# Softmax attentions by head pairs, and a regrouped tail of the recurrence, in an eight-layer transformer kernel

## The chip, the cores and the metric

The program runs on one NeuronCore of one Trainium2 chip. The metric is device microseconds of the whole kernel, one launch. Before the change the median of three timed runs is 3063.12 us (3058.28 to 3063.68).

## The reference

Two stacks of layers act on x of 256 tokens by 1024 features, in float32. The four layers of the first stack are `x += ffn/2; x += mixer; x += ffn/2`, each with an RMS norm; the mixers are, in this order, a gated recurrence (HGRN2), a neighbourhood attention (NA), a latent attention (MLA) and the recurrence again. The second stack has a linear recurrence, a gated convolution ffn, a stick-breaking attention and another ffn. The change touches the first stack's mixers:

```python
# NA, 16 heads of 64; a row is 64 tokens, T = 4 rows, so every query sees all 256 keys
s = einsum(q_r, k_blk) * scale
s = where(col_mask, s + bias, NEG_INF)      # bias = rpb by row and column offset
p = softmax(s);  o = einsum(p, v)
# MLA, 16 heads, 96 query/key features, 64 value features, q and k RMS-normed and rotated
s = einsum(q_b, k) * scale;  p = softmax(s);  o = einsum(p, v)
# HGRN2, 8 heads of 128: a decayed causal attention, forward and backward
o = rms_norm(o, g_norm) * silu(g);  y = o @ w_out
```

## The kernel before

Matmuls by weights are split in three (`three`, L621 to L623): weights and activations are each cut into a high part in fp32r and a low remainder. Weights stream by units of 128x1024 through six raw buffers (SP queue); ScalarE makes the high part of a unit (L1246) and VectorE the low part (L1747), into seven split buffers. Both engines follow a hand-written order: `splits(tile)` and `ahead(n)` say up to which unit they go before the next piece of their other work, and each engine runs strictly in the order of its program. All dependences are semaphores. PSUM has eight banks; 0 to 3 are called Wk and 4 to 7 Y, and Y also collects the output of a sublayer.

`hgrn` works on four pairs of heads. In a pair, nine scores (`score`, L874) run along a ladder of decay levels: TensorE makes the score of level i, VectorE doubles the decayed keys and queries (`double`, L1986) and keeps part of the score (`keep`, L1997), ScalarE copies the keys (`facing_keys`, L1419), then the score of the next level can run. Beside the first three pairs TensorE has the input products of the next pair (`half_product`), one half after each score. The last pair has none; there the output product of the pairs 0 and 1 stands (`pair_out`, four halves after the scores 3 to 6), and behind the ladder `output`, `squares_summed`, pair 2, and after the norm (`normed`, L2004 and L2007) and its split (L1767, L1769) pair 3 in `last_tile`.

`na` makes eight units of q and k (`f_product`), each followed by `mean_squares` (L938) and by `flip` (L981), a matmul that reverses the order of the 64 partitions of each bias block; VectorE copies it back (L2109), GpSimd then adds the column mask per head (L573). Four products for v follow, then `attention`. `mla` is alike, without bias; its last part is eight `queries` with `query_squares`.

`attention` goes head by head on TensorE: scores of head i (L944, two matmuls), the four 128x128 transposes of head i-2 (L960), values of head i-3 (L971, two matmuls onto 64 partitions of a bank that two heads share). Fp32 matmuls show as two records each, transposes as one. VectorE, per head: in NA scale and bias (L2120), maximum (L2084), its negation (L2085), reciprocal of the sum of the head before (L2077), the multiplication of that head's 256x256 exponentials by it (L2079, twice 128x256), and every second head the split of the output (L1767, L1769). ScalarE: the copy of the transposed probabilities (L1487) and the exponentials with their sum (L1496). `w_out` waits for the last head's split.

## Time and profile before

| | |
|---|---|
| median of 3 timed runs | 3063.12 us (3058.28 to 3063.68) |
| profiled execution | 3055.57 us, span 3053.8 us |
| PE busy, share of the span | 93% |
| DVE, ACT, POOL | 66%, 47%, 3% |
| granted TensorE clock, mean | 0.969 |
| DMA | 478 MB, 157 GB/s |

PE is TensorE, DVE VectorE, ACT ScalarE, POOL GpSimd. The profile is of one execution. Its page has the busy time by engine and the chain of work that ended last; the trace behind it can be asked for the instructions of a stretch in order of time, for who waited for whom, and for busy time and granted clock by stretch. A granted clock of 1.00 is 2.4 GHz, 0.50 is 1.2 GHz. Times in the rows are microseconds from the start of the span. The recurrence runs from about 228 to 445 us and again from about 1933 to 2150, NA from 820 to 994, MLA's attention from 1472 to 1519.

### The profile page before, as it was taken

How to read it: one execution, taken by the hardware profiler on the slowest of the kernel's cores; microseconds unless marked ns; L12 is line 12 of the kernel's file. 1: busy time of each engine (PE TensorE's matmuls, PEld its weight loads, DVE VectorE, ACT ScalarE, POOL GpSimd, SP SyncE). 2: the span in 40 equal slices, each digit the busy share in tenths (PEclk: the TensorE clock that was granted, in tenths of full speed). 3: DMA queues.
4: the chain of work that ended last, by engine and by line, in shares of the span. 5: the costliest groups of instructions: out<-in, count | busy, mean ns of one | idle time of the engine just before them, and what ended most of it. 6: DMA issues, size and time to landing. Idle time of an engine off the chain costs nothing.

```text
span 3053.8 us, 46734 instructions
## 1 busy us (share of the span) xinstructions
PE 2855.1 (93%) x19701; PEld 2639.7 (86%) x19701; DVE 2002.9 (66%) x2615; ACT 1426.9 (47%) x1904; POOL 98.7 (3%) x148
## 2 busy tenths in 40 slices
PE   7999979999988999999999999997999699896998
PEld 6999869999975999998799999996999599794897
DVE  5667766565657666557665665776656677746777
ACT  4445544444444544445554444554444444453443
POOL 0000000000002000001100000000000100000000
PEclk9999999999999999999999999998999899997999
DMA  7654326675541565553256566432664456442562
GB/s 227 188 161 138 112 82 215 186 207 186 159 145 49 184 184 183 182 167 93 94 181 186 166 200 186 132 125 69 199 185 154 138 173 200 152 156 65 166 192 98
DMA packets 404726, 478.41 MB, mean 157 GB/s; under 512 B 16555, under 2 KB 331653, under 8 KB 404517
## 3 DMA queue, kind: packets, MB, share of 16 engines
q1 hardware_dynamic: 400944, 467.33, 48.8%
q0 software_dynamic: 1776, 6.77, 0.8%
q8 instruction: 155, 2.54, 0.3%
q10 hardware_dynamic: 1796, 1.33, 0.1%
q14 instruction: 55, 0.44, 0.0%
HBM read 474.32 MB, written 1.05 MB: 156 GB/s over the span
## 4 chain that ended last, share of the span: by engine, by line
PE 82%; DVE 10%; ACT 4%; issue 3%; ACTq 0%; DVEq 0%
PE Wk L621 17%; PE Wk L623 16%; PE Wk L622 16%; PE Y L621 9%; PE Y L622 9%; PE Y L623 9%; DVE w_lo L1747 2%; DVE work L1986 1%; ACT w_hi L1246 1%; PE Y L971 1%; PE Y L874 1%; PE Y L726 1%; PE Wk L944 1%; PE Wk L960 0%; PE Wk L874 0%
## 5 line engine op out<-in xcount | busy, mean ns | idle before, releaser
L1747 DVE TENSOR_TENSOR w_lo<-ring,w_hi 128x1024 fp32r<-128x1024 f32 (+2 forms) x910 | 1070.4, 1200 | 690.1 <-ACT w_hi L1246 643.7
L621 PE MATMUL Wk<-xT_hi,w_hi 128*128 128x256 f32 x4320 | 1233.3, 285 | 21.0 <-DVE xT_lo L1786 17.7
L623 PE MATMUL Wk<-xT_hi,w_lo 128*128 128x256 f32 x4320 | 1225.6, 284 | 0.0
L622 PE MATMUL Wk<-xT_lo,w_hi 128*128 128x256 f32 x4320 | 1225.6, 284 | 0.0
L1246 ACT ACTIVATE w_hi<-ring 128x1024 fp32r<-128x1024 f32 (+1 forms) x894 | 906.8, 1039 | 645.0 <-PE Wk L623 431.7
L621 PEld LDWEIGHTS Wk<-xT_hi,w_hi 128*128 128x128 f32 x4320 | 832.2, 193 | 28.2 <-issue 14.8
L622 PEld LDWEIGHTS Wk<-xT_lo,w_hi 128*128 128x128 f32 x4320 | 832.4, 193 | 4.7 <-issue 0.9
L623 PEld LDWEIGHTS Wk<-xT_hi,w_lo 128*128 128x128 f32 x4320 | 831.9, 193 | 0.0
L621 PE MATMUL Y<-w_hi,hid_hi 128*128 128x512 f32 x904 | 353.5, 391 | 4.3 <-DVE hid_lo L1840 4.3
L622 PE MATMUL Y<-w_lo,hid_hi 128*128 128x512 f32 x904 | 352.1, 389 | 0.0
L623 PE MATMUL Y<-w_hi,hid_lo 128*128 128x512 f32 x904 | 350.9, 388 | 0.0
L621 PEld LDWEIGHTS Y<-w_hi,hid_hi 128*128 128x128 f32 x904 | 170.1, 188 | 37.6 <-DVE hid_lo L1840 5.2
L623 PEld LDWEIGHTS Y<-w_hi,hid_lo 128*128 128x128 f32 x904 | 169.8, 188 | 35.8
L622 PEld LDWEIGHTS Y<-w_lo,hid_hi 128*128 128x128 f32 x904 | 170.2, 188 | 30.8
L1315 ACT ACTIVATE hid_hi<-work 128x512 fp32r<-128x512 f32 x112 | 70.8, 632 | 241.9 <-DVE work L1838 241.9
L621 PE MATMUL Y<-w_hi,xT_hi 128*128 128x512 f32 (+1 forms) x288 | 108.8, 378 | 31.9 <-DVE xT_lo L1769 15.6
L1840 DVE TENSOR_TENSOR hid_lo<-work,hid_hi 128x512 fp32r<-128x512 f32 x112 | 77.6, 693 | 78.3 <-ACT hid_hi L1315 78.3
L623 PE MATMUL Y<-w_hi,xT_lo 128*128 128x512 f32 (+1 forms) x288 | 104.9, 364 | 0.0
L622 PE MATMUL Y<-w_lo,xT_hi 128*128 128x512 f32 (+1 forms) x288 | 104.9, 364 | 0.0
L621 PEld LDWEIGHTS Y<-w_hi,xT_hi 128*128 128x128 f32 x288 | 56.9, 197 | 43.9 <-DVE xT_lo L1769 18.5
L1419 ACT ACTIVATE work<-work 128x512 f32<-128x512 f32 x56 | 38.0, 678 | 108.5 <-DVE work L1986 108.5
L1986 DVE TENSOR_TENSOR work<-work 128x512 f32<-128x512 f32 x112 | 79.2, 754 | 12.4 <-PE Wk L874 10.5
(283 smaller groups left out, 2829.1 us busy)
## 6 DMA issues: line engine op xcount, KB each, us to landing
ring<-in_ffn_w_gu SPq DMA_DIRECT2D x352, 512.0 KB, 4.4
ring<-in_ffn_w_down SPq DMA_DIRECT2D x224, 512.0 KB, 4.4
ring<-in_ffn_w_up SPq DMA_DIRECT2D x96, 512.0 KB, 5.9
ring<-in_hg_w_in SPq DMA_DIRECT2D x80, 512.0 KB, 3.6
ring<-in_na_w_in SPq DMA_DIRECT2D x24, 512.0 KB, 4.5
ring<-in_hg_w_out SPq DMA_DIRECT2D x16, 512.0 KB, 3.6
ring<-in_lru_w_in SPq DMA_DIRECT2D x16, 512.0 KB, 4.4
ring<-in_kv_w SPq DMA_DIRECT2D x16, 512.0 KB, 4.5
```

The source lines that it names most:

```text
L621: pe.matmul(o, l_hi, r_hi, start=first, stop=False)
L622: pe.matmul(o, l_hi, r_lo, start=False, stop=False)
L623: return pe.matmul(o, l_lo, r_hi, start=False, stop=last)
L726: mm = pe.transpose(part_bank(tt, n)[:, k * P:(k + 1) * P], x[:, tt, a:a + P], ident)
L874: mm = pe.matmul(o[:, (2 * hh + st) * P:(2 * hh + st + 1) * P], dk, dq, start=True, stop=True)
L944: mm = pe.matmul(o[:, tt * T:(tt + 1) * T], q_of(i)[:, tt * P:(tt + 1) * P], k_of(i), start=True, stop=True)
L1246: act.activation(*both[-1], ACT.Copy).then_inc(hi_done, 1)
L1315: act.activation(hid_hi[:, h, :], ff_hid[:, h, :], ACT.Copy).then_inc(hidden_high, 1)
L1419: act.activation(hg_dk[:, i % 2, :].rearrange("p (n h b) -> p n h b", h=2, b=P >> l), facing(Q, l, 0), ACT.Copy).then_inc(dk_ready, 1)
L1747: ins = dve.tensor_tensor(l, r, h.bitcast(F32), ALU.subtract)
L1840: dve.tensor_tensor(hid_lo[:, h, :], ff_hid[:, h, :], hid_hi[:, h, :].bitcast(F32), ALU.subtract)\
L1986: dve.tensor_tensor(a, a, other_block(l, which), ALU.mult) .then_inc((k_doubled, q_doubled)[which], 1)
```

## The change

Attention. A new `softmax_attention` takes the place of `attention` in NA and MLA. VectorE no longer multiplies the exponentials: it makes a 128x128 diagonal of the inverse sums (the identity times the reciprocal), two per head. TensorE then multiplies the exponentials, as stationary operand, by the diagonal, which turns and scales at once, four real fp32 matmuls where four transposes stood. Scores and values go by pairs of heads, alternating between the two. The order on TensorE is: scores of pair g, values of pair g-2, turning of the two heads of pair g-1. The score banks are four (0, 1, 6, 7), the exponentials and the turned copies have four buffers. The maximum is negated by the reduction itself. The first pair's scores, maxima and exponentials move ahead of the last input products (NA: behind the second v product; MLA: ahead of the last queries). `w_out` starts its first half when seven of eight splits are done.

NA's bias. The flip matmuls and the copies are gone. The queries are stored in reverse order of tokens within 128, the bias load and the column mask are adapted, and the split of the output writes in reverse again.

Recurrence. The four halves of the output product of the pairs 0 and 1 go after the scores 0, 2, 4 and 6 of the last pair, in the order (0,0), (1,0), (0,1), (1,1), and the weight units are reordered for it. The split of pair 0 moves to pair 2 (into another tile), of pair 1 to level 0 and of pair 2 to level 5. The last pair's weight splits are spread over the levels, three units of the next sublayer are split ahead of the last norm, and VectorE doesn't split any more between it and the residual. In the other pairs the weight split of a level is moved ahead of the other work of that level. Squares of pair 2 move ahead by some instructions.

```diff
-MS_BANKS = (4, 4, 4, 2)
+A_BANKS = (0, 1, 6, 7)
+MS_BANKS = (4, 4, 0, 2)
+HALVES_LAST = (0, 0, 1, 1, 2, 2, 3, 4, 5)
 LEVELS = 8
 SCORES = LEVELS + 1
 HALVES_AHEAD = 4
@@ -61,8 +63,8 @@
 
 class Const:
...
-                    t_product(*out_of(t0, j), first=j == 0)
+                    if j == 0 and subs[s][0] in ("na", "mla"):
+                        for n in range(2):
+                            pe.wait_ge(s_saved, saves_before(s) + 7 + n)
+                            y_half(out_of(t0, j), n, first=True)
+                    else:
+                        t_product(*out_of(t0, j), first=j == 0)
...
                     pe.wait_ge(o_split, Q0 + j + 1)
-                    if j == 0 and n == 0:
-                        pe.wait_ge(g_saved, Q0 + HG_PAIRS)
-                        pe.wait_ge(o_ready, Q0 + HG_PAIRS - 1)
-                    y_half(out_of(base[s] + 5 * HG_PAIRS, j), n, first=j == 0)
+                    if j == 0:
+                        pe.wait_ge(*((o_ready, Q0 + HG_PAIRS - 1) if n else (g_saved, Q0 + HG_PAIRS)))
+                    t = base[s] + 5 * HG_PAIRS
+                    a = (t + j, pair_of(hid_hi, j), pair_of(hid_lo, j)) if j < 2 else out_of(t, j)
+                    y_half(a, n, first=j == 0)
...
-                        if last and 3 <= i < 7:
-                            pair_out((i - 3) // 2, (i - 3) % 2)
+                        if last and i in (0, 2, 4, 6):
+                            pair_out(i // 2 % 2, i // 4)
...
+            def scores_of_pair(g, q_of, k_of):
+
+                for tt in range(TT):
+                    for h in (2 * g, 2 * g + 1):
+                        mm = pe.matmul(bank(A_BANKS[h % 4])[:, tt * T:(tt + 1) * T],
+                                       q_of(h)[:, tt * P:(tt + 1) * P], k_of(h), start=True, stop=True)
+                        if tt:
+                            mm.then_inc(s_psum, 1)
+
+            def softmax_attention(s, q_of, k_of, at_v, at_p, at_pT):
+
+                h0, s0, pairs = heads_before(s), saves_before(s), NA_H // 2
+
+                def turned(h):
+
+                    pe.wait_ge(s_prob, 2 * (h0 + h + 1))
+                    if h >= 2:
+                        pe.wait_ge(s_turned_sb, h0 + h - 1)
+                    for kk in range(TT):
+                        for tt in range(TT):
+                            mm = pe.matmul(bank(2 + h % 2)[:, kk * T + tt * P:kk * T + (tt + 1) * P],
+                                           at_p[:, h % 4, tt, kk * P:(kk + 1) * P], inv_diag[:, h % 2, tt, :],
+                                           start=True, stop=True)
+                    mm.then_inc(s_turned, 1)
+
+                def values(g):
+
+                    pe.wait_ge(s_turned_sb, h0 + 2 * g + 2)
+                    if g >= 2:
+                        pe.wait_ge(s_saved, s0 + g - 1)
+                    for kk in range(TT):
+                        for hh in range(2):
+                            h = 2 * g + hh
+                            mm = pe.matmul(bank(4 + g % 2)[64 * hh:64 * hh + 64, 0:T], at_v[:, kk, 64 * h:64 * h + 64],
+                                           at_pT[:, h % 4, kk, :], start=(kk == 0), stop=(kk == 1))
+                            if kk:
+                                mm.then_inc(s_out, 1)
+
+                for g in range(pairs + 2):
+                    if 1 <= g < pairs:
+                        scores_of_pair(g, q_of, k_of)
+                    if g >= 2:
+                        values(g - 2)
+                    if 1 <= g <= pairs:
+                        turned(2 * g - 2)
+                        turned(2 * g - 1)
...
-                    flip(i - 1)
-                pe.wait_ge(na_flipped, NA_H // 2)
                 for j in range(4):
                     if j >= 2:
                         pe.wait_ge(p_v, v0 + TT * (j - 1))
                     v_product(base[s] + 8 + j, bank(4 + j % 2))
-                pe.wait_ge(p_out, u0 + 8)
+                    if j == 1:
+                        pe.wait_ge(p_out, u0 + 8)
+                        scores_of_pair(0, part(na_q), part(na_k))
                 pe.wait_ge(p_v, v0 + 8)
-                attention(s, NA_H, part(na_q), part(na_k), NA_D, na_v, na_p, na_pT)
-                pe.wait_ge(s_saved, saves_before(s) + 8)
+                softmax_attention(s, part(na_q), part(na_k), na_v, na_p, na_pT)
                 w_out(s, base[s] + 12)
...
+                    if i == 7:
+                        pe.wait_ge(k_fin, 8)
+                        scores_of_pair(0, q_of, k_of)
                     queries(i)
                     if i < 2:
                         key_squares(2 + i)
                     if i:
                         query_squares(i - 1)
-                pe.wait_ge(k_fin, 8)
-                for h in range(3):
-                    scores_of(h, q_of, k_of)
                 query_squares(7)
                 pe.wait_ge(q_fin, 8)
-                attention(s, MLA_H, q_of, k_of, MLA_V, ml_v, ml_p, ml_pT, ahead=3)
-                pe.wait_ge(s_saved, saves_before(s) + 8)
+                softmax_attention(s, q_of, k_of, ml_v, ml_p, ml_pT)
                 w_out(s, t0 + 15)
...
+                        if last and i == 1:
+                            squares_of(p_ - 1)
                         if i < LEVELS - 1:
                             facing_keys(p_, i + 1)
                         if i in (0, LEVELS - 1, LEVELS):
                             keep(p_, i)
                         if i == 1:
                             g_sigmoid(Q)
-                        if p_ and i == 3 - 2 * last:
+                        if not last:
+                            ahead(HALVES_AHEAD + 10 * (p_ + 1) + i, s)
+                        if p_ and i == 3 and not last:
                             squares_of(p_ - 1)
                         if p_ and i == 5 - 3 * last:
                             roots(p_ - 1)
@@ -1463,7 +1530,9 @@
                                 one_minus(Q + 1)
                             elif i == LEVELS:
                                 save_values(p_ + 1)
-                        ahead(HALVES_AHEAD + 10 * (p_ + 1) + i, s)
+                        else:
+                            ahead(HALVES_AHEAD + 38 + HALVES_LAST[i], s)
+                ahead(10 * HG_PAIRS + 10, s, over=True)
                 squares_of(HG_PAIRS - 1)
                 roots(HG_PAIRS - 1)
...
+                for g in range(1, pairs + 1):
+                    if g < pairs:
+                        exps(2 * g)
+                    turned(2 * g - 2)
+                    turned(2 * g - 1)
+                    if g < pairs:
+                        exps(2 * g + 1)
...
                 def split_pair(pp):
                     dve.wait_ge(o_ready, Q0 + pp + 1)
-                    split_out(2 * pp, 2, hg_o[:, pp, :], (o_high, Q0 + pp + 1), o_split)
+                    if pp >= 2:
+                        split_out(2 * pp, 2, hg_o[:, pp, :], (o_high, Q0 + pp + 1), o_split)
+                        return
+                    dve.tensor_copy(hid_hi[:, pp, :], hg_o[:, pp, :]).then_inc(o_high, 1)
+                    dve.wait_ge(o_high, Q0 + pp + 1)
+                    dve.tensor_tensor(hid_lo[:, pp, :], hg_o[:, pp, :], hid_hi[:, pp, :].bitcast(F32), ALU.subtract)\
+                        .then_inc(o_split, 1)
 
                 splits(base[s] + 2)
                 dve.wait_ge(r_ready, norms_before(s) + 1)
@@ -2035,13 +2138,14 @@
                             save_g(p_)
                         elif i == 2:
                             gate_of(p_)
-                        if last and i in (1, 2):
-                            split_pair(i - 1)
+                        if p_ == HG_PAIRS - 2 and i == 5:
+                            split_pair(0)
+                        if last and i in (0, 5):
+                            split_pair(1 + i // 5)
                         if p_ and i == 6 - 3 * last:
                             normed(p_ - 1)
-                            if last:
-                                split_pair(2)
                         if not last:
+                            ahead(HALVES_AHEAD + 10 * (p_ + 1) + i, s)
                             if i == 4:
                                 save_z(p_ + 1)
                             elif i == 6:
@@ -2052,11 +2156,13 @@
                             elif i == LEVELS:
                                 both_ways(p_ + 1)
                                 multiply_blocks(Q + 1, LEVELS - 1)
-                        ahead(HALVES_AHEAD + 10 * (p_ + 1) + i, s)
+                        else:
+                            ahead(HALVES_AHEAD + 38 + HALVES_LAST[i], s)
+                ahead(10 * HG_PAIRS + 10, s, over=True)
                 normed(HG_PAIRS - 1)
                 split_pair(HG_PAIRS - 1)
...
+            def softmax_attention(s, scores, split=1):
+
+                h0, g0 = heads_before(s), saves_before(s)
+
+                def inverse_sums(h):
+
+                    dve.wait_ge(s_exp, 2 * (h0 + h + 1))
+                    r = a_stat(3, h)
+                    step(dve.reciprocal(r, a_stat(2, h)))
+                    if h >= 2:
+                        dve.wait_ge(s_turned, h0 + h - 1)
+                    for tt in range(TT):
+                        dve.tensor_scalar(inv_diag[:, h % 2, tt, :], ident, r[:, tt:tt + 1], None, ALU.mult)\
+                            .then_inc(s_prob, 1)
+
+                for i in range(1, NA_H + 4):
+                    if 2 <= i < NA_H:
+                        scores(i)
+                    if i <= NA_H:
+                        inverse_sums(i - 1)
+                    if i >= 5 and i % 2:
+                        g = (i - 5) // 2
+                        dve.wait_ge(s_out, h0 + 2 * g + 2)
+                        o = bank(4 + g % 2)[:, 0:T].rearrange("p (a t) -> p a t", a=split)
+                        split_out(g, 1, o, (s_high, g0 + g + 1), s_saved)
+
+            def scores_max(h, src):
+                dve.tensor_reduce(a_stat(1, h), src, AX.X, ALU.max, negate=True).then_inc(s_max, 1)
...
-                    o = (na_q if i < 4 else na_k)[:, 2 * (i % 4):2 * (i % 4) + 2, :].rearrange("p a b -> p (a b)")
-                    dve.scalar_tensor_tensor(o, bank(S_BANKS[i % 3]), na_gain[:, i // 4:i // 4 + 1], na_rs[:, u % 2, :],
-                                             ALU.mult, ALU.mult).then_inc(p_out, 1)
-                dve.wait_ge(na_flipped, NA_H // 2)
```

## Rows read from the trace of the kernel before

**Rows 1.** Page: busy time by engine; chain that ended last, by engine
```profile
PE 2855.1 (93%) x19701; PEld 2639.7 (86%) x19701; DVE 2002.9 (66%) x2615; ACT 1426.9 (47%) x1904; POOL 98.7 (3%) x148
...
PE 82%; DVE 10%; ACT 4%; issue 3%; ACTq 0%; DVEq 0%
```
**Rows 2.** NA's products: chain in order of time (start, us); waits (total, times, longest)
```profile
833.16 0.84 PE Y L981 x2
...
PE Y L621 <- DVE work L2109: 4.1, 1, 4.1
```
**Rows 3.** NA's attention, TensorE in order of time: start, us, [idle before <-releaser]
```profile
910.33 1.14 PE L944 MATMUL Wk<-work 64*128 64x256 f32 x8 [1.02 <-ACT work L1524]
...
917.09 1.11 PE L960 MATMUL Wk<-cst,work 128*128 128x128 f32 x4 [4.80 <-DVE work L2079]
...
968.54 1.84 PE L971 MATMUL Y<-work 128*64 128x256 f32 x8
971.35 0.50 PE L621 MATMUL Y<-w_hi,xT_hi 128*128 128x512 f32 x1 [0.98 <-DVE xT_lo L1769]
```
**Rows 4.** The same attention, VectorE and GpSimd in order of time, one pair
```profile
950.00 0.41 DVE L1767 CAST xT_hi<-Y 128x256 fp32r<-128x256 f32 x1
...
950.78 0.68 DVE L2120 SCALAR_TENSOR_TENSOR xn<-Y,xn 128x512 f32<-128x512 f32 x1
...
952.22 0.17 DVE L2085 TENSOR_SCALAR stat<-stat 128x2 f32<-128x2 f32 x1
...
952.49 1.50 DVE L2079 TENSOR_SCALAR work<-work,stat 128x256 f32<-128x256 f32 x2
953.92 0.68 DVE L2120 SCALAR_TENSOR_TENSOR xn<-Wk,xn 128x512 f32<-128x512 f32 x1
...
957.05 0.41 DVE L1767 CAST xT_hi<-Y 128x256 fp32r<-128x256 f32 x1
...
952.47 1.37 POOL L573 TENSOR_TENSOR xn<-work,cst 128x256 f32<-128x256 f32 x2 [2.54 <-DVE stat L2085]
```
**Rows 5.** The same attention by stretch: length, busy (instructions) by engine, PEclk
```profile
935.00:971.00 36.00, 28.02 (x128) 15.74 (x126) 32.36 (x73) 18.70 (x52) 10.46 (x16) 1.00 0.00 1
```
**Rows 6.** MLA's attention, TensorE in order of time
```profile
1479.03 1.09 PE L960 MATMUL Wk<-cst,xn 128*128 128x128 f32 x4 [3.22 <-DVE xn L2079]
...
1498.32 1.13 PE L944 MATMUL Wk<-work 128*128 128x256 f32 x4
...
1499.29 0.60 PE L960 MATMUL Wk<-cst,xn 128*128 128x128 f32 x4
...
1499.82 1.08 PE L971 MATMUL Y<-work 128*64 128x256 f32 x4
...
1500.82 1.13 PE L944 MATMUL Y<-work 128*128 128x256 f32 x4
...
1518.67 0.50 PE L621 MATMUL Y<-w_hi,xT_hi 128*128 128x512 f32 x1 [0.98 <-DVE xT_lo L1769]
```
**Rows 7.** The recurrence, TensorE in order of time: second pair, then last pair
```profile
303.03 1.05 PE L874 MATMUL Y<-work 128*128 128x128 f32 x8
303.84 0.36 PE L621 MATMUL Wk<-xT_hi,w_hi 128*128 128x256 f32 x1
...
317.30 1.53 PE L874 MATMUL Y<-work 128*128 128x128 f32 x8 [1.95 <-ACT work L1419]
...
389.89 2.07 PE L899 MATMUL Y<-xn,cst 128*128 128x512 f32 x2 [5.14 <-ACT xn L1425]
...
402.17 0.77 PE L621 MATMUL Y<-w_hi,xT_hi 128*128 128x512 f32 x1 [6.12 <-DVE work L2007]
...
422.67 1.99 PE L887 MATMUL Wk<-work 128*128 128x256 f32 x8 [0.69 <-ACT work L1406]
...
432.43 0.50 PE L621 MATMUL Y<-w_hi,xT_hi 128*128 128x512 f32 x1 [1.38 <-DVE xT_lo L1769]
```
**Rows 8.** The recurrence's end, VectorE in order of time
```profile
436.84 1.28 DVE L1803 SCALAR_TENSOR_TENSOR x<-Y,x 128x512 f32<-128x512 f32 x2
```

More of the change, by code:

```diff
@@ L1754, in splits, with ahead @@
                     nxt[0] += 1
-            def ahead(n, s):
-                while nxt[0] <= nth[split_units_of(s)[0]] + n and split_units[nxt[0]][0] < end[s]:
+            def ahead(n, s, over=False):
+                while nxt[0] <= nth[split_units_of(s)[0]] + n and (over or split_units[nxt[0]][0] < end[s]):
                     low(split_units[nxt[0]])
```

155 lines of the change are left out of this document (89 added, 66 removed).

## Prediction

> **What bounds the kernel now.** I read the page first: TensorE is busy for 93% of the span, and 82% of the chain that ended last is its own work [rows 1]. So an edit pays where it takes work off TensorE, or ends a stretch in which TensorE stands. Then the trace, for TensorE alone, through the three places the change touches: which record comes late, and who released it. Last the granted clock by stretch.
>
> NA's products: each of the eight units ends with a flip of 0.84 us on TensorE, and after the last flip the v products wait 4.1 us, since VectorE copies the last block back only after two weight splits [rows 2]. The reader is to see two costs of one edit: the matmul, and the wait behind it.
>
> NA's attention: from the end of the wait for v to the output product, 910.33 to 971.35, 61.0 us [rows 3]. TensorE stands 4.80 us ahead of the first transposes, since scale, maxima and exponentials begin only then. In steady state VectorE is the bound: from one output split to the next, a pair of heads, 957.05 - 950.00 = 7.05 us [rows 4], while over 36 us TensorE was busy 28.0 at full clock [rows 5].
>
> MLA's attention: no bias, so VectorE has room and TensorE is the bound. A head is scores 0.97, transposes 0.53, values 1.00, starts from 1498.32 to 1500.82 = 2.50 us [rows 6]. There is 3.22 us of standing ahead of the first transposes.
>
> Recurrence, twice the same (the second 1703.4 us later, with the same gaps): in the last pair TensorE has nothing between the levels until the norm of pair 2 is split: gaps of 5.14 and 6.12 us, and the ladder ends at 422.67 [rows 7]. In the first three pairs there is a gap where VectorE waits for a split that ScalarE makes after a sigmoid: 1.95 us at 317.30 in the second pair [rows 7].
>
> **The change part by part.**
>
> *Flips.* 8 x 0.84 = 6.7 us of TensorE, all on the path, and the 4.1 us wait: 10.8 us. What is late next is the weight split of the second v tile; it is made during the last q/k units, one v tile ahead, so nothing. The reverse order itself I cost at nothing on VectorE: four writes of queries and the splits of the output run with the same number of elements, by a stride of -1. No row shows a negative stride; bounds 0 and, if each element took twice as long, 16 halves of splits of 0.41 us [rows 4] = +6.6 us. I take 0: only the order changes, not the amount. GpSimd's first bias adds move some 50 us ahead, beside work that has slack.
>
> *NA's attention.* VectorE per head now, by starts [rows 4]: scale and maximum 952.22 - 950.78 = 1.44; negation and reciprocal 952.49 - 952.22 = 0.27; the two multiplications 953.92 - 952.49 = 1.43; per pair 0.78 for the output split. 2 x 3.14 + 0.78 = 7.06. The multiplications take 1.43 us for 2 x 256 elements, and GpSimd's two adds run from 952.47 for 1.37 us: each multiplication ends just behind an add. So halving its elements hardly shortens it; what shortens is that GpSimd starts with the maximum, now 0.08 earlier by the negation (0.27 less a reciprocal of about 0.19) and 0.19 earlier against the multiplications. I take 0.28 per head, a pair 6.5; bounds: nothing (7.05), and the adds no longer in the way (the diagonals in about a fourth of 1.43 each, pair 5.0). TensorE's pair would be scores 0.95 (two row groups of 64 at once; the first two heads' eight records take 1.14 us including a tail of 0.2, where four alone take 1.13 in MLA [rows 3, 6]), values 1.0, turning 1.7, in all 3.65: below 6.5.
>
> The start: the first two heads are ready when v ends. The scores of pair 1 follow at once (0.95), VectorE takes them up 0.15 later and is busy from 1.1 to the end. It has seven pairs of 6.5 = 45.5; minus 1.8, since heads 14 and 15 have no adds beside them, minus 0.8 for a split that comes later: 44.0 us to the last diagonal. Then turning 0.85, copy 0.75, values 1.0: 46.6 to 46.7, and the output product's first half starts at once, since it needs seven splits of eight (this takes the 0.98 us of rows 3, and 1.0 for the first tail in MLA). 61.0 - 46.7 = 14.3 us less. Against it the pair scores of heads 0 and 1, 0.95, now ahead of the wait. And TensorE stands more: 2.8 of 6.5 us. Clock: behind the 4.80 us gap it was at half, four transposes took 1.11 instead of 0.60 [rows 3, 6]; with 28.0 of 36 us busy it stayed at full [rows 5]. The new gaps are 1 to 2 us. If at half, the pair is TensorE's with scores 1.8, values 1.8, turning 3.5 = 7.1 instead of 6.5: 8 x 0.6 = 5, plus 2 in the output product. I take 3 for it. NA's attention: 14.3 - 0.95 - 3 = 10.4 us.
>
> *MLA's attention.* Turning is a real fp32 matmul: four of 128x128 with eight records cost 303.84 - 303.03 = 0.81 us [rows 7] against 0.53 for transposes. Pair: scores 2 x 0.91 = 1.8, turning 2 x 0.9 with its waits = 1.8, values. The values of the two heads go to different halves of the array's columns. If they run side by side, 1.0; if one after the other, 2.0. The row nearest: eight records at 968.54 take 1.84, where two blocks of four would take 1.00 + 1.08 = 2.08, although the second four had to wait for ScalarE's copy [rows 3]. I take 1.0: pair 4.6 against 5.0, 8 x 0.4 = 3.2 us; with 2.0 it is 5.6, a loss of 4.8. Start: the wait added is that VectorE's maxima and ScalarE's exponentials of heads 0 and 1 stand ahead of the last queries' square and copy. They need the pair scores (1.8 us on TensorE, moved ahead of 4.6 us of query product that covers them), so they are done first, and nobody waits. The third head's scores (0.97) leave the start, the pair's stay. What is late next is VectorE, which still has two weight splits and the last query means ahead of the first diagonal: first turning at about 1478.4 instead of 1479.03, second at 1479.8, then steady. End: 1513.1 against 1518.67, in all 5.6 us. Bounds -2 and +8.
>
> *Recurrence, last pair.* From the scores of level 1 to `output` of pair 3: 422.67 - 383.26 (end of `output` of pair 2; its scores follow in order) = 39.4 us. In this stand the gaps of 5.14, 6.12 and 0.69 and two of about 1.4, and the half clock behind them (the square sum of rows 7 takes 2.07, twice its time at full clock), about 3.7 in all; together 18.5 us. With halves of the output product, 2.8 us each by my count of twelve records, after levels 0, 2, 4 and 6 I walk the ladder by the durations of the trace: level 1 now starts at 386.0, later by one half; level 2 at 389.2 (before 391.8), level 3 at 392.8, then a wait of 3.0 for VectorE, which has keep, gate and one split; level 4 at 396.8, its half waits 1.2 for the norm of pair 2 (same bank); levels 5 to 8 at 401.7, 404.0, 407.7, 410.2; `output` at 411.8. Gain 10.9 us, bounds 7 and 12. I take off 1.9 for half clock behind the 3.0 us: 9.0.
>
> *Recurrence, tail.* `last_tile` starts 432.43 - 422.67 = 9.76 behind `output`; same chain, but ScalarE has three more splits ahead of the squares: they fit, +0.2. The residual add starts at 436.84 behind four splits [rows 8], although it needs only the first six records of `last_tile`, about 1.6 us behind 432.43; now at once: -2 to -2.8. But one unit of the next sublayer isn't split yet, and VectorE comes to it only after the norm's row: TensorE stands about 2.0 there. Net 0, bounds -2.5 and +2.5.
>
> *Recurrence, pairs 0 to 2.* The weight split of a level goes ahead of the other work. Today the split waits while ScalarE does a sigmoid; the gap of 1.95 should shrink. Cost now per transition, by my estimate 4.5 us: the gap, as much in two smaller ones and half clock behind (1.53 instead of 1.05 for the score at 317.30 [rows 7]). VectorE's load per level stays, and it is close to TensorE's, so the gain is between 0 and 4.5; I take 1.5, six transitions in all 9 us, bounds 0 and 27. In the third one VectorE also gets a split of pair 0, 1.1 us, inside this.
>
> Both recurrences: 2 x 9.0 + 9 = 27 us.
>
> **Sum.** 10.8 + 10.4 + 5.6 + 27 = 53.8 us. Profiled execution: 3055.6 - 53.8 = 3001.8. It is 7.5 us below the median of the timed runs, and for that the sum gives 3063.1 - 53.8 = 3009.3.
>
> **A rule of the Trainium skill against it.** *TensorE: Matmul & The Clock Gate*, Part 3, says that a weight load overlaps with matmuls in flight only when its row group differs. By that rule the paired values, all on 128 rows, would not overlap, and MLA gives 3009 + 8 = 3017. The row at 968.54 speaks for some overlap (1.84, not 2.08), but no row shows an alternating pair; the case is part of rival 2. Part 4 of that page says that transposes don't count as activity for the clock as matmuls do. By that rule NA, whose transposes become matmuls, would rather keep its clock, and the 3 us are not lost: 3006.
>
> **The rivals.**
> 1. *More comes back in the recurrence.* The transitions give 3.5 each instead of 1.5 (12 us) and the last pair no half clock (4), NA none (3): 3009 - 19 = 2990. For: the gaps have one cause. Against: VectorE's load.
> 2. *The pairing doesn't pair, and gaps cost clock.* Values one after the other in MLA +8, NA at half clock throughout +4, last pairs 2 x 3: 3009 + 18 = 3027. For: NA's idle share of TensorE grows from 22% (8.0 of 36 us [rows 5]) to over 40%.
> 3. *Slower: TensorE at half clock through all three.* Mechanism: TensorE's work per gap is cut up so that the clock doesn't come back. Price: MLA's pair from 4.6 to 9.2, 8 x 4.6 = 37; NA 7; the last pairs' 18 us of matmuls twice, 2 x 18 - 4 = 32 (halves, scores, square sums); in all 76: 3085. It makes the kernel slower once over 7 tenths of these stretches are at half. Against: MLA's TensorE is without gaps, and full clock held at the 28.0 of 36 us of rows 5.
> 4. *No change*: gains of the last pair taken back by the late units at the next sublayer, and the reversed strides dear. 3057 to 3069.
>
> **How the numbers follow.** Forecast 0.70 (2998 to 3022), rival 1 0.11, rival 2 0.14, rival 3 0.03, rival 4 0.02. The range of 8 in 10 leaves out half of rival 1 and the far end of rival 2: 2989 to 3028. A measurement of this kernel tells 0.2%, 6 us, from no change. Faster 0.95, same 0.02, slower 0.03.
>
> **What would show it.** Flips: no L981-like record, v products right behind the last square sum, 10.8 us earlier. NA: a pair in 6.5 us on VectorE, the diagonals still as long as GpSimd's adds, first turning within 1.2 us of the end of the wait for v, 47 to 50 us to the output product. MLA: pair 4.6, values of a pair with eight records in about 1.1. Last pair: no gap above 3.0 us, 28 to 31 us instead of 39.4. Transitions: the gap at level 5 to 6 from 1.95 to about 1. Wrong, if VectorE's diagonals run without waiting (NA much faster), if the granted clock in NA or in the last pair is at half, or if the first sublayer behind the recurrence stands for its weights by more than 2 us.

## The result and the profile after

The kernel after takes 2992.67 us (2990.69 to 2993.27) against 3063.40 us (3058.28 to 3063.80) of the kernel before in the same comparison: a ratio of 0.9772, 95% interval 0.9755 to 0.9789, so 70.7 us less. Forecast were 3009 us, with a range from 2989 to 3028. The profiled execution after takes 2992.14 us, 0.5 below its median. The mean granted clock rose from 0.969 to 0.975.

The page after, busy time by engine and the last chain by engine; [rows 1] are the same of before. TensorE's share of the chain rises from 82% to 86%, VectorE's falls from 10% to 8%.

```profile
PE 2826.6 (95%) x19813; PEld 2629.9 (88%) x19813; DVE 1989.4 (67%) x2591; ACT 1425.3 (48%) x1904; POOL 99.9 (3%) x148
...
PE 86%; DVE 8%; ACT 3%; issue 2%; ACTq 0%; POOL 0%; DVEq 0%
```

NA after, TensorE in order of time (start, us, [idle before <-releaser]), which answers [rows 3]. L1005 are scores, L1021 the turnings by a diagonal, L1034 values, L639 is the output product. The rows are the paired scores in the midst of the v products, the scores that end the wait for v, the first two turnings, the longest gap in steady state, a pair's values and the output product.

```profile
867.69 1.13 PE L1005 MATMUL Wk<-work 64*128 64x256 f32 x8
...
881.46 1.14 PE L1005 MATMUL Y<-work 64*128 64x256 f32 x8 [0.93 <-ACT work L1616]
882.52 1.16 PE L1021 MATMUL Wk<-junk,work 128*128 128x128 f32 x8
885.57 1.16 PE L1021 MATMUL Wk<-junk,work 128*128 128x128 f32 x8 [1.89 <-DVE junk L2192]
...
897.60 1.57 PE L1021 MATMUL Wk<-junk,work 128*128 128x128 f32 x8 [2.08 <-DVE junk L2192]
...
901.11 1.30 PE L1034 MATMUL Y<-work 128*64 128x256 f32 x8
...
929.10 0.50 PE L639 MATMUL Y<-w_hi,xT_hi 128*128 128x512 f32 x1
```

The same on VectorE and GpSimd, which answers [rows 4]: the two diagonals of a head last 1.38 us, and they end with GpSimd's two adds, 1.32 us from 896.13. Below it the window of these pairs (length; busy of PE, PEld, DVE, ACT, POOL; granted clock): VectorE is busy for 14.51 of 15 us, and the clock is 0.89.

```profile
896.13 1.32 POOL L591 TENSOR_TENSOR xn<-work,cst 128x256 f32<-128x256 f32 x2 [2.27 <-DVE stat L2207]
896.16 1.38 DVE L2192 TENSOR_SCALAR junk<-cst,stat 128x128 f32<-128x128 f32 x2
...
895.00:910.00 15.00, 10.74 (x69) 7.45 (x67) 14.51 (x29) 7.22 (x24) 6.20 (x10) 0.89 0.01 2
```

MLA after, TensorE, which answers [rows 6]: scores of the second pair at half clock (3.63 us; a later pair's take 1.89), then turnings of a pair in 2.09, the last values of eight records in 1.08, the output product.

```profile
1433.92 3.63 PE L1005 MATMUL Y<-work 128*128 128x256 f32 x8
1437.34 2.09 PE L1021 MATMUL Wk<-junk,xn 128*128 128x128 f32 x16
...
1472.22 1.08 PE L1034 MATMUL Y<-work 128*64 128x256 f32 x8 [0.69 <-ACT work L1579]
1473.23 0.50 PE L639 MATMUL Y<-w_hi,xT_hi 128*128 128x512 f32 x1
```

The recurrence after, TensorE, which answers [rows 7] (L897 are scores, L910 is `output`, L639 to L641 are products by weights): the score that stood 1.95 us now follows at once, then five rows of the last pair, and the wait of the next sublayer for a weight unit.

```profile
312.47 1.16 PE L897 MATMUL Y<-work 128*128 128x128 f32 x8
...
385.43 1.42 PE L897 MATMUL Wk<-work 128*128 128x128 f32 x8 [2.54 <-ACT work L1482]
387.61 0.77 PE L639 MATMUL Y<-w_hi,hid_hi 128*128 128x512 f32 x1 [0.77 <-issue]
388.17 0.63 PE L640 MATMUL Y<-w_lo,hid_hi 128*128 128x512 f32 x1
...
401.87 1.13 PE L897 MATMUL Wk<-work 128*128 128x128 f32 x8 [1.65 <-DVE work L2083]
403.69 3.44 PE L910 MATMUL Wk<-work 128*128 128x256 f32 x8 [0.69 <-ACT work L1469]
...
433.75 0.39 PE L639 MATMUL Wk<-xT_hi,w_hi 128*128 128x256 f32 x1 [1.73 <-DVE w_lo L1842]
```

### The profile page after: what moved, and what is told of

It reads as the page before. It is cut to its first block, busy times and chain, and to the rows that moved or that the text cites. A ratio compares the mean times of both kernels' runs of the same rounds, so it can differ in the third digit from the quotient of the medians.

```text
span 2990.3 us, 46983 instructions
## 1 busy us (share of the span) xinstructions
PE 2826.6 (95%) x19813; PEld 2629.9 (88%) x19813; DVE 1989.4 (67%) x2591; ACT 1425.3 (48%) x1904; POOL 99.9 (3%) x148
## 4 chain that ended last, share of the span: by engine, by line
PE 86%; DVE 8%; ACT 3%; issue 2%; ACTq 0%; POOL 0%; DVEq 0%
PE Wk L639 17%; PE Wk L641 17%; PE Wk L640 17%; PE Y L639 9%; PE Y L640 9%; PE Y L641 9%; DVE w_lo L1842 2%; PE Y L897 1%; DVE work L2083 1%; PE Y L744 1%; ACT w_hi L1309 1%; PE Wk L1021 1%; PE Wk L897 0%; DVE stat L1922 0%; DVE junk L2192 0%
## 5 line engine op out<-in xcount | busy, mean ns | idle before, releaser
L639 PE MATMUL Wk<-xT_hi,w_hi 128*128 128x256 f32 x4320 | 1232.8, 285 | 24.5 <-DVE xT_lo L1883 17.8
L641 PE MATMUL Wk<-xT_hi,w_lo 128*128 128x256 f32 x4320 | 1225.2, 284 | 0.0
L639 PEld LDWEIGHTS Wk<-xT_hi,w_hi 128*128 128x128 f32 x4320 | 831.5, 192 | 32.2 <-issue 14.9
L641 PEld LDWEIGHTS Wk<-xT_hi,w_lo 128*128 128x128 f32 x4320 | 831.2, 192 | 0.0
L639 PE MATMUL Y<-w_hi,hid_hi 128*128 128x512 f32 x936 | 369.2, 394 | 6.4 <-DVE hid_lo L1937 4.6
L640 PE MATMUL Y<-w_lo,hid_hi 128*128 128x512 f32 x936 | 366.5, 392 | 0.0
L641 PE MATMUL Y<-w_hi,hid_lo 128*128 128x512 f32 x936 | 365.4, 390 | 0.0
L639 PEld LDWEIGHTS Y<-w_hi,hid_hi 128*128 128x128 f32 x936 | 177.5, 190 | 41.5 <-DVE hid_lo L1937 5.5
L641 PEld LDWEIGHTS Y<-w_hi,hid_lo 128*128 128x128 f32 x936 | 176.9, 189 | 37.6
L640 PEld LDWEIGHTS Y<-w_lo,hid_hi 128*128 128x128 f32 x936 | 177.6, 190 | 32.2
L639 PE MATMUL Y<-w_hi,xT_hi 128*128 128x512 f32 (+1 forms) x256 | 93.4, 365 | 14.2 <-DVE xT_lo L1866 14.2
L640 PE MATMUL Y<-w_lo,xT_hi 128*128 128x512 f32 (+1 forms) x256 | 90.4, 353 | 0.0
L641 PE MATMUL Y<-w_hi,xT_lo 128*128 128x512 f32 (+1 forms) x256 | 90.3, 353 | 0.0
L1951 DVE TENSOR_TENSOR work<-Wk,r_row 128x512 f32<-128x512 f32 x88 | 60.7, 690 | 35.0 <-PE Wk L641 35.0
```

What stands on the lines that cost most here:

```text
L639: pe.matmul(o, l_hi, r_hi, start=first, stop=False)
L640: pe.matmul(o, l_hi, r_lo, start=False, stop=False)
L641: return pe.matmul(o, l_lo, r_hi, start=False, stop=last)
L1951: dve.tensor_tensor(wide(ff_silu[:, h, :]), wide(bank(2 * h)), r_wide(2), ALU.mult)\
```

## The experiments

To compare traces I cut each into sublayers, at TensorE's first transposes of each norm. Lengths in us; the columns are the kernel before in two executions, three kernels with one part of the change, and the kernel after. "Weights ahead" is the weight split moved ahead of its level, "all of recurrence" the whole part of the change in the recurrence, "bias" NA's bias part. Sublayers that are not shown differ by 0.5 at most. A measured time below that has no range comes from one execution.

| sublayer | before, 1st | before, 2nd | weights ahead | all of recurrence | bias | after |
|---|---|---|---|---|---|---|
| recurrence 1 | 225.2 | 225.3 | 214.4 | 205.5 | 225.4 | 205.3 |
| ffn behind it | 189.2 | 190.7 | 190.8 | 191.5 | 190.7 | 191.5 |
| NA | 174.8 | 176.6 | 174.8 | 178.3 | 163.1 | 150.1 |
| MLA | 169.4 | 169.6 | 170.8 | 169.6 | 169.6 | 166.2 |
| recurrence 2 | 225.1 | 225.2 | 213.1 | 205.3 | 225.2 | 202.7 |
| ffn behind it | 189.2 | 190.6 | 189.2 | 191.5 | 190.6 | 191.5 |
| lru | 111.5 | 110.9 | 111.3 | 111.7 | 110.9 | 111.7 |
| gated ffn | 220.9 | 223.6 | 220.8 | 221.0 | 223.7 | 221.1 |
| last gated ffn | 228.1 | 228.1 | 228.0 | 228.1 | 229.3 | 229.6 |

**The kernel before once more.**

> The kernel before, unchanged, profiled once more. Its first profiled execution took 3055.6 us, 8 us below its timed median, while the profiled executions of the kernel after and of three partial kernels lie within 3 us of theirs. If that one execution was a fast one, this lies near 3063 and the stages show where the 8 us are; if profiling itself makes this kernel faster, it is again near 3056. It also shows how far a stage whose code is the same differs between executions: the runs so far say 0.0 to 0.4 us in most, and steps of 1.4 to 3.5 us in a few.

It took 3063.23 us, and all executions of this kernel on record lie between 3055.57 and 3065.74. So the first profiled execution was a quick one and not the usual one. The difference sits in four places, one to three us each: both ffns behind a recurrence, NA and the gated ffn. It is clock: over these four the mean granted clock was 1.00, 1.00, 0.95 and 0.97 in the first execution and 0.99, 0.99, 0.94 and 0.96 in the second, and the same 15 us behind the recurrence were granted 1.00 in the first (first line) and 0.89 in the second.

```profile
430.00:445.00 15.00, 11.49 (x68) 9.48 (x67) 13.30 (x19) 8.28 (x16) 1.52 (x4) 1.00 0.44 141
```

```profile
430.00:445.00 15.00, 11.54 (x54) 9.36 (x52) 12.35 (x16) 8.10 (x15) 0.00 (x0) 0.89 0.44 141
```

In these places TensorE has just stood, and whether the stretch behind is granted the full clock changed from one execution to the next. A stage next to gaps can therefore be read only to 1.5 to 3.5 us (NA, with the same code, takes 174.8 to 178.3 in the table), one without gaps (the other ffns) to 0.1.

**The weight split ahead of its level, alone.**

```diff
                         if i == 1:
                             g_sigmoid(Q)
+                        if not last:
+                            ahead(HALVES_AHEAD + 10 * (p_ + 1) + i, s)
...
-                        ahead(HALVES_AHEAD + 10 * (p_ + 1) + i, s)
+                        if last:
+                            ahead(HALVES_AHEAD + 10 * (p_ + 1) + i, s)
```

This is ScalarE's side; VectorE's is alike.

> The kernel before with one edit: in the first three pairs of the recurrence the weight split of a level stands ahead of that level's other work on ScalarE and VectorE. The forecast had 1.5 us for each of six transitions, 9 us in all, and the last pair as before. The rival (more comes back in the recurrence) has 3.5 each, 21 us in all; the trace after the change gives 11.7 us for the first recurrence (level 0 of the last pair starts at 368.9 instead of 380.6), so 23 in all. If the gain came from elsewhere in the change (the weight units in another order, the square sum of pair 2 moved), it is nearer to 9.

Measured: 3036.11 us (3035.16 to 3040.17) against 3064.33, ratio 0.9909 (0.9895 to 0.9924), 28.2 us less. The two recurrences are 10.9 and 12.1 us shorter than in the second execution of before, together 23.0, or 3.8 a transition. The forecast had 9, the rival 21. The rest of the 28 lies in sublayers whose code is the same, above all the gated ffn (2.8), NA (1.8) and one ffn (1.4), where the two executions of before differ by as much.

**The whole recurrence part, alone.**

> The kernel before with the whole of the change in the recurrence and nothing else. By the forecast's sum 27 us less than before. By what the trace after the change shows for the same stages (37.5 us shorter, and 4.6 us longer in the two sublayers behind them) 33 us less, if the parts don't act on each other. Rival: part of the gain in the recurrence was a gift of another part (clock or transfers), then the two recurrences together are shorter by less than 35 us here.

Measured: 3022.99 us (3021.08 to 3025.33), ratio 0.9864 (0.985 to 0.9879), 41.3 us less. The two recurrences are 19.8 and 19.9 us shorter than in the second execution of before. Together that is more than 35, so the gain is not a gift of another part. The 33 us expected were too low: by the table the recurrences of the kernel after are 42.3 us shorter than in the first execution of before and the ffns behind them 4.6 longer, so 37.7 was already the net. Against the kernel above, the last pair and its tail give 8.9 and 7.8 us. In the kernel after one of the two recurrences is 202.7 instead of 205; the same step comes and goes in kernels whose recurrence is the same (202.7 and 202.7 with the values by head, 202.8 and 205.8 with the diagonals by a product of tensors), and it is the clock of the last pair: from 370 to 420 us it is 0.90 in the kernel after and 0.97 in those two, and `output`, 1.99 us in [rows 7], takes 3.44 after.

**The bias part, alone.**

> The kernel before with the bias part alone: no reversing matmuls and no copies back, queries stored and output split in reverse order. The forecast has 10.8 us less (eight matmuls of 0.84 us and the wait of 4.1), the reversed writes at nothing; if each reversed element took twice as long, 16 halves of splits cost 6.6 us more and the gain is 4.2. The attention itself is VectorE's and keeps its pair of 7.05 us by the first theory.

Measured: 3051.08 us (3050.14 to 3052.01), ratio 0.9956 (0.9939 to 0.9972), 13.2 us less; NA is 11.7 or 13.5 us shorter, by which execution of before one takes. VectorE's pair of heads is still 7.05 us (924.24 to 931.28), so the gain lies ahead of the attention. The reversed writes cost nothing that shows: a reversed write of queries takes 0.75 us, as one in order does, and the 128x256 CAST of the output split 0.41.

The recurrence (41.3 us) and the bias (13.2) leave 16.2 of the 70.7 us to the attentions, which have no kernel of their own; the table gives 13.0 for NA (bias to after) and 3.4 for MLA.

**Values of a pair head by head.**

```diff
-                    for kk in range(TT):
-                        for hh in range(2):
+                    for hh in range(2):
+                        for kk in range(TT):
```

> The kernel after with one edit: the four value matmuls of a pair run head by head, two for one head and then two for the other, instead of alternating between the two halves of the array's columns. If they run side by side only because they alternate, a pair's eight records take 1.8 to 2.1 us instead of 1.08 and MLA's attention is 6 to 8 us longer, NA's 0 to 3 (VectorE bounds it). If the order doesn't matter, both stay within 0.5 us, and the pairing of the values was not what the change gained.

Measured: 2990.22 us; NA 150.1 and MLA 166.3, as after. In MLA a pair's values take the same time in the other order:

```profile
1439.25 1.09 PE L1034 MATMUL Y<-work 128*64 128x256 f32 x8
```

One head's values take 1.08 us too [rows 6]. So two heads on the two halves of the array's columns run side by side in either order. What the change needed was that they follow each other at all; before, another head's scores and transposes stood between.

**GpSimd's adds cut short.**

```diff
-                            pool.tensor_tensor(na_b[:, h % 2, tt, :].rearrange("p (r c) -> p r c", r=4), R, m,
-                                               ALU.add).then_inc(s_biased, 1)
+                            o = na_b[:, h % 2, tt, :].rearrange("p (r c) -> p r c", r=4)
+                            if h >= 2:
+                                o, R, mm = o[:, 0:1, 0:8], R[:, 0:1, 0:8], m[:, 0:1, 0:8]
...
+                            pool.tensor_tensor(o, R, mm, ALU.add).then_inc(s_biased, 1)
```

> The kernel after, but GpSimd's bias adds of NA are cut to 8 of 256 columns from the third head on (so the bias of those heads is left as it was in the buffer). If the adds are what VectorE's diagonals wait for (1.38 us for two beside them, 0.48 in MLA), the diagonals take 0.5, the pair goes from 6.6 to between 4.8 and 5.2 and NA is 9 to 13 us shorter. If the diagonals are long for another reason, the pair stays at 6.6. If TensorE or ScalarE is next at once, the pair ends at 5.5 or more.

This kernel leaves out most of the bias of 14 of NA's 16 heads and serves only to time the stage. Measured: NA 139.6 us, 10.4 less (2981.50 us in all). Pairs follow by 4.61 us (894.45 to 899.06), and the diagonals take 0.48:

```profile
898.64 0.37 POOL L596 TENSOR_TENSOR xn<-work,cst 128x8 f32<-128x8 f32 x2 [1.54 <-DVE stat L2211]
898.67 0.48 DVE L2196 TENSOR_SCALAR junk<-cst,stat 128x128 f32<-128x128 f32 x2
```

**The diagonals by a product of two tensors.**

```diff
-                    for tt in range(TT):
-                        dve.tensor_scalar(inv_diag[:, h % 2, tt, :], ident, r[:, tt:tt + 1], None, ALU.mult)\
-                            .then_inc(s_prob, 1)
+                    dve.tensor_tensor(inv_diag[:, h % 2, :, :], ident.unsqueeze(1).broadcast_to([P, TT, P]),
+                                      r.unsqueeze(2).broadcast_to([P, TT, P]), ALU.mult).then_inc(s_prob, 2)
```

> The kernel after, with the two diagonals of a head made by one multiplication of two tensors (identity by the inverse sums, both repeated) instead of two multiplications by a scalar column. Scale and bias (0.68 us, two tensors) ran beside the adds without getting longer, so this form may not wait for them: about 0.35 to 0.45 us for 256 elements, a NA pair of 4.9 to 5.4 instead of 6.6, NA 8 to 12 us shorter; MLA within 0.5 us, since TensorE bounds it. Rival: any read of two tensors beside GpSimd waits too, and NA stays within 1 us.

Measured: NA 144.7 us, 5.4 less (2987.21 in all), and a pair of 5.5, so the 8 to 12 us and the 4.9 to 5.4 a pair were missed. The theory held by half: the form takes 0.88 us beside the adds, and 0.43 where the adds are over (915.09).

```profile
900.81 1.51 POOL L591 TENSOR_TENSOR xn<-work,cst 128x256 f32<-128x256 f32 x2 [0.85 <-DVE stat L2206]
900.89 0.88 DVE L2191 TENSOR_TENSOR junk<-cst,stat 128x256 f32<-128x256 f32 x1
...
915.09 0.43 DVE L2191 TENSOR_TENSOR junk<-cst,stat 128x256 f32<-128x256 f32 x1
```

It ends 0.28 us behind the first of the two adds (901.77 against 901.49), the other form 0.08 behind the second (897.54 against 897.46): it waits for one add, the other form for both. The Trainium skill, *SBUF — State Buffer*, "Who interferes with whom", says that VectorE and GpSimd share one pair of ports, that the second of them waits until the first instruction is over, and that both `tensor_scalar` and a `tensor_tensor` with two inputs in SBUF take part, a reduction not. The rows agree with all three (the maximum keeps its 0.69 us beside the adds).

**The adds later.**

```diff
                             pool.wait_ge(s_max, heads_before(s) + h - 1)
+                        if h >= 3:
+                            pool.wait_ge(s_prob, 2 * (heads_before(s) + h - 2))
```

> The kernel after, with one wait more on GpSimd: the bias adds of a NA head start only when the diagonals three heads back are made, not when the maximum two heads back is. The adds (1.37 us) then should run beside scale and maximum (0.68 and 0.69, which do not get longer beside them), and the diagonals find GpSimd idle and take 0.48: the pair from 6.6 to 4.6 to 5.0, NA 9 to 11 us shorter, as with the adds cut short (10.4). If the adds slip so that scale waits for them, or they still touch the diagonals, NA is 0 to 5 us shorter.

Measured: 2980.39 us, NA 139.7, as with the adds cut short. A pair is again 4.61 us. The adds now begin behind the diagonals and run beside scale and maximum, which keep their 0.69 us:

```profile
900.66 0.48 DVE L2194 TENSOR_SCALAR junk<-cst,stat 128x128 f32<-128x128 f32 x2
901.06 0.69 DVE L2241 SCALAR_TENSOR_TENSOR xn<-Y,xn 128x512 f32<-128x512 f32 x1
901.29 1.32 POOL L593 TENSOR_TENSOR xn<-work,cst 128x256 f32<-128x256 f32 x2 [1.37 <-DVE junk L2194]
901.78 0.69 DVE L2209 TENSOR_REDUCE stat<-xn 128x2 f32<-128x512 f32 x1
```

The clock comes back too, as it does in the two kernels before this one (1.00 over the same 20 us in both). The 20 us from 895 in the kernel after, then in this one:

```profile
895.00:915.00 20.00, 15.18 (x93) 10.25 (x91) 19.37 (x38) 9.44 (x30) 7.95 (x12) 0.84 0.01 2
```

```profile
895.00:915.00 20.00, 18.16 (x137) 13.46 (x136) 18.78 (x53) 13.10 (x41) 8.62 (x14) 1.00 0.01 2
```

**MLA turned by transposes again.**

```diff
-                                           start=True, stop=True)
+                                           start=True, stop=True) \
+                                if subs[s][0] not in ('mla',) else \
+                                pe.transpose(bank(2 + h % 2)[:, kk * T + tt * P:kk * T + (tt + 1) * P],
+                                             at_p[:, h % 4, tt, kk * P:(kk + 1) * P], ident)
...
+                    if subs[s][0] in ('mla',):
...
+                            dve.tensor_scalar(o, o, r[:, tt:tt + 1], None, ALU.mult).then_inc(s_prob, 1)
```

> The kernel after, with MLA's probabilities again multiplied by the inverse sums on VectorE and turned by transposes instead of by matmuls with a diagonal; pairs, buffers and order stay. By the forecast's prices a head's turning goes from 0.94 to 0.53 us on TensorE, which bounds MLA: the pair from 4.73 to 3.9 and MLA 6 to 7 us shorter, unless VectorE (two maxima, two multiplications, a split: some 3.9 us a pair) or ScalarE (four exponentials and two copies: 4.3 us a pair) becomes the bound; then the gain is 3 us. Rival: the clock falls, since transposes take the place of matmuls, and MLA is no shorter or longer.

Measured: 2984.69 us, MLA 159.2, 7.0 less. Pairs follow by 3.76 us (1442.34 to 1446.10) instead of 4.73 (later ones by up to 3.84), and the granted clock from 1440 to 1465 us stays 1.00, so the rival falls:

```profile
1442.34 1.08 PE L1037 MATMUL Y<-work 128*64 128x256 f32 x8
1443.35 1.09 PE L1025 MATMUL Wk<-cst,xn 128*128 128x128 f32 x8
1444.28 1.89 PE L1005 MATMUL Wk<-work 128*128 128x256 f32 x8
1446.10 1.08 PE L1037 MATMUL Y<-work 128*64 128x256 f32 x8
```

**The tail of the recurrence.** One more `ahead(10 * HG_PAIRS + 11, s, over=True)` behind `roots` on ScalarE and behind the last `split_pair` on VectorE, and

```diff
-                pair_out(2, 0)
-                squares_summed(HG_PAIRS - 1)
+                pair_out(2, 0, lambda: squares_summed(HG_PAIRS - 1))
```

This puts the square sum between the two row blocks of that half of the output product.

> The kernel after, with two edits at the end of the recurrence: the weight unit that the next sublayer stands for (1.73 us) is split behind the last norm instead of behind the norm's row of the next sublayer, and the square sum of the last pair stands between the two halves of the output product's half ahead of it. By the first theory the sublayer behind the recurrence is 1.7 us shorter each time and the recurrence 1.0 to 1.4 each time (the gap ahead of the last tile), 5 to 6 us in all. Rival: the half clock behind these gaps is only moved, and the steps of 1.4 to 2.6 us that the same stages showed between executions hide it: 0 to 3 us.

Measured: 2986.62 us, 6.0 less than the median after. The ffns behind the recurrences are 189.5 us each, 2.0 less: the wait of 1.73 us is gone, as expected. The recurrences are 202.7 and 201.1, against 205.3 and 202.7; the gap of 1.38 us ahead of the last tile is gone, but one of 0.91 now stands ahead of the square sum, and the clock steps are as large as the rest. Where `output` runs at full clock, as in the second recurrence of the kernel after, it is 12.6 us from `output` to the next norm's transposes without the edit and 12.4 with it, so that second edit brings some 0.2 us and not the 1.0 to 1.4 expected.

**Adds later, transposes in MLA and the tail together.**

> The kernel after with three edits together: GpSimd's adds later, MLA turned by transposes, and the tail of the recurrence. From the single runs: 10.4 (short adds) + 7.0 (MLA) + 5 (tail, expected) = 22 us less than after, 2970. If the gains act on each other through the clock, 2975 to 2982.

Measured: 2971.42 us (2969.72 to 2972.89) against 3063.09, ratio 0.9702 (0.9688 to 0.9715): 21 us faster than the kernel after, where 2970 was expected. NA is 139.6, MLA 160.0, the ffns behind the recurrence 189.5, and both recurrences are at 204.4.

## Why the prediction was right, and where it was not

The direction and the range held; the middle was 16 us too high. Of the three parts of rival 1 (2990 us) two came true, the transitions and NA's clock; the third, a last pair without half clock, did not. Measured against the second execution of before, the terms are (a recurrence is cut here at the first score of its last pair and at that pair's `output`; the tail is what lies behind, with the change of the ffn):

| term | forecast | measured |
|---|---|---|
| flips and their wait | 10.8 | 13.5 |
| NA's attention (bias kernel to after) | 10.4 | 13.0 |
| MLA | 5.6 | 3.4 |
| transitions of pairs 0 to 2 | 9.0 | 23.2 |
| last pairs, without the tail | 18.0 | 16.2 |
| tail of both | 0 | 1.3 |

Together that is 70.6 us. Sublayers that the change does not touch moved as well and nearly cancel: the gated ffn is 2.5 us shorter, a step that the two executions of before show between them too (2.7), while lru is 0.8 and the last gated ffn 1.5 longer. The middle missed by 16 us above all because the transitions are worth 14 us more than forecast; flips and NA add 5, the tails 1, and MLA and the last pairs take 4 back, so misses in both directions partly hid each other.

*Transitions: the term that was mis-sized.* I put what the misplaced split costs now at 4.5 us a transition, and took 1.5 of it, because VectorE's load per level was "close to TensorE's". It gave back 3.8 to 3.9. The mechanism was right, the discount for VectorE's load was wrong: over 40 us of the second pair VectorE was busy for 31.0 before and 33.9 after, so there was room. The window of before, then of after:

```profile
295.00:335.00 40.00, 36.73 (x282) 35.46 (x281) 31.03 (x44) 22.16 (x30) 0.00 (x0) 0.96 0.36 115
```

```profile
295.00:335.00 40.00, 39.41 (x315) 38.27 (x314) 33.85 (x47) 23.53 (x33) 0.00 (x0) 1.00 0.41 125
```

The first line could have been read before predicting: 9 of 40 us idle on VectorE, and a clock of 0.96 that comes back with the gaps. The kernel with this edit alone (23.0 us) shows that the gain is this edit's.

*Flips.* The mechanism held: the v products start right behind the last square sum. The term left out the half clock behind the wait of 4.1 us: over the 20 us behind it (884 to 904 in the first execution, 886 to 906 in the second) the granted clock was 0.91 and 0.85. NA is 11.7 us shorter against the quick execution and 13.5 against the usual one.

*NA's attention.* The pair was right (6.5 forecast, 6.4 to 6.6 measured), and so was its reason: the diagonals are as long as the adds, which two kernels show by taking the adds away and by moving them. From the end of the wait for v the first turning follows in 1.06 us (881.46 to 882.52; forecast within 1.2), where it took 6.8 before, and the output product in 47.6 (to 929.10; forecast 47 to 50). What was mis-sized is the 3 us put down for the clock. It did fall, to 0.89 where [rows 5] have 1.00, so the reason for 3006 us, that NA keeps its clock, did not come true. But VectorE bounds the pair either way, and the walk without any loss gave 46.6 to 46.7: it cost 1 us at most. What I had as a bound, adds out of the way and 5.0 a pair, was to be had by one wait: 4.61. Which parts of the new order NA's 13 us come from was not separated: no kernel has the pairs and the early first scores with transposes in NA.

*MLA.* The pair came to 4.73 instead of 4.6, 1.0 us in all, and the second pair's scores ran at half clock (3.63 instead of 1.89), 1.7 us; together 2.7, a little more than the 2.2 that are missing against the forecast. The price of turning (0.9 against 0.53) was nearly right (0.94), and MLA with transposes shows what it costs: 7.0 us, of which 0.6 is clock (the second pair's scores take 3.01 us there). There the diagonal lengthens the bound engine to relieve one that is not bound.

*Values side by side.* By the rule that I cited (the Trainium skill, *TensorE: Matmul & The Clock Gate*, Part 3) they would have taken 2.0 us; 1.08 was measured. [rows 1] already spoke against it: nearly all weights of this kernel fill all 128 rows, and yet weight loads were busy for 86% of the span beside 93% for matmuls. The same page of the Trainium skill, "Why this matters for your kernels", says that outputs on different partitions use separate groups of columns and run concurrently; the rows agree with that line.

*Last pair.* The walk was right in kind: gaps of 1.41, 2.54, 1.45 and 1.65 us and none of 5 or 6. The stretch forecast at 28 to 31 us instead of 39.4 took 32.3 in the first recurrence (371.34 to 403.69) and 31.2 in the second, so this sign was missed by a little. The half of the output product behind the 2.54 us took 5.25 us (387.61 to 392.86) where the one behind level 0 took 2.8: 2.5 us for half clock, where I had taken 1.9.

*Tail.* The residual came earlier, as costed (it starts 1.7 us behind `last_tile` instead of 4.4), and the late unit cost 1.73 us. From `output` to the next norm it is 0.8 and 2.3 us less. Each ffn is 0.9 us longer than in the usual execution, 2.3 than in the quick one, and 1.2 shorter than the former once the unit is early.

*The scale.* All terms were read from a quick execution, and the sum was then carried to the median by adding the 7.5 us between the two. That is no fixed offset but clock lost in the usual executions, partly in the stages that the change shortens (1.8 us in NA). Profiled against profiled the forecast was 3001.8 us and the result 2992.14.

*The rivals.* Rival 2 falls with the values at 1.08 us and with NA, where half clock cost 1 us at most and TensorE stood for 4.3 of the 15 us from 895, 28% and not over 40%. Rival 3 falls since MLA's pair is at full clock from the third pair on (scores 1.89 us), and rival 4 since the tail is no loss and the reversed writes cost nothing.

## What to carry to other kernels

Before discounting a gain because another engine is loaded, read that engine's busy time over the stage: 31 of 40 us leave room. When VectorE and GpSimd work in one loop, look whether a VectorE instruction ends with a GpSimd one; moving GpSimd's start to the stretch of VectorE work that does not wait gave 10 us for one wait more. A trick that trades one engine for another (turning by a diagonal) lost 7 us in the stage where the relieved engine was not the bound. Before a gain is carried from a profile to the median, profile the same kernel a second time.

## What the runs showed of the hardware

- Two fp32 multiplications of 128x128 by a scalar column on VectorE take 0.48 us alone and 1.38 beside GpSimd's adds; one product of two tensors of 128x256 takes 0.43 and 0.88. Scale and bias with the scores in PSUM (0.68) and the maximum (0.69) do not change.
- Value matmuls of two heads on 64 columns each take 1.08 us for eight records, alternating or not, as one head's four records do.
- Turning four 128x128 blocks in fp32 takes 0.94 us by matmuls with a diagonal and 0.53 by transposes.
- A write of VectorE with a stride of -1 takes as long as one in order (0.75 us for 128x512).
- The same code in the same place was granted 1.00 or 0.89 of the clock in two executions, behind a stretch in which TensorE stood; such steps moved single stages by 1.4 to 3.5 us, and the two executions of the kernel before differ by 7.7 us.
